# First stage of a three-block layer: modulation columns split between TensorE sums up front and VectorE sums beside the projections

## Chip, cores, metric

One core of one Trainium2 chip runs the whole program once. The metric is device microseconds of that execution (lower is better); the number compared is the median of several executions.

## What is computed

The reference is a long layer in float32 on 1024 tokens of width 1024. Only its beginning matters here: an adaptive norm whose shifts, scales and gates are columns of one product, the input projections, a gated linear attention, and later a second norm and a feed-forward part that use the remaining columns.

```python
def adaln(cond, w, b):
    return jax.nn.silu(cond) @ w + b          # w: 1024 x 6144, b: 6144
...
sh1, sc1, gt1, sh2, sc2, gt2 = jnp.split(adaln(c, w_ada, b_ada), 6, axis=-1)
csh1, csc1, ... = jnp.split(adaln(c_ctx, w_ada, b_ada), 6, axis=-1)   # only these two are used
hc = modulate(rmsnorm(ctx, g_pre_mix), csh1, csc1)      # h * (1 + scale) + shift; ctx: 256 tokens
hx = modulate(rmsnorm(x, g_pre_mix), sh1, sc1)
yx = token_mixers(hx @ w_in, ...)                       # projections, gates, linear attention
x = x + gt1 * rmsnorm(yx @ w_out, g_post_mix)
hx = modulate(rmsnorm(x, g_pre_ffn), sh2, sc2)
x = x + gt2 * rmsnorm(conv_ffn(hx, ...), g_post_ffn)
```

Two further blocks (windowed attention with a recurrent mixer, and a mixture of experts) follow and are not touched.

## The kernel before

The program is a row of stages. A stage gives each engine its instruction list; it ends when every engine has ended its list, and the next begins then. Within a stage the engines are ordered by semaphores that are waited for by hand-written counts. Each engine runs its list in order, and DMAs are issued from the lists of SyncE (SP) and ScalarE (ACT) in order too.

**`stage_modulation` (L228).** All 6144 columns of the product are made, spread over the 128 partitions, in `mod_rows`: eight rows of 1024, named `R_SH1, R_G1, R_GP1, R_SH2, R_G2, R_GP2, R_CSH, R_CG`. `w_ada` comes in 12 chunks of 512 columns (2 MB each, `ada_weights`, four buffers). Partition p holds eight of the 1024 input rows, `k` = 0 to 7. For each chunk VectorE forms a chain over `k` = 0 to 6 (L341 once, L345 six times), ScalarE scales the eighth part (L296), and TensorE sums over the partitions with an all-ones matrix and adds the bias (L373, L374, L375: three float32 matmuls with 512 moving columns, the last with one row). ScalarE copies the result from PSUM (L302). The first four chunks are done twice, for `c` and for `c_ctx` (L323). SP reloads a buffer when its `sum_mm` count is there. ScalarE's queue brings in the masks, the small parameters, `ctx`, `x` and four gain rows (L293). At the end TensorE turns the parameters (L398), VectorE copies them (L353) and multiplies the gains into five rows (L359, L362).

**`stage_norm_turn` "norm1" (L403)** normalises ten tiles of tokens and turns them with TensorE; it begins when the first stage has ended.

**`stage_project_mix` (L535).** First 40 steps `q` (five groups of eight): SP loads a 128 x 512 slice of `w_in` (`w_tm`, L594, two buffers; load `q` waits for `tm_low` of `q-2`), ScalarE and VectorE split it in a high and a low part (L208, L213), and TensorE does 12 matmuls with it (6 in the third group, which has two token tiles). In steps 9 to 12, 17 to 20 and 25 and 26, VectorE also copies a finished tile from PSUM (L684). Then 17 kinds `n` of 128 output columns each (`w_cm`, L601, one buffer), with 48 matmuls of 512 columns per kind for the later ones. PSUM banks 6 and 7 are unused by kinds 5 and later.

**`stage_gates` (L735), `stage_gla` (L857).** The second runs two context chunks and then eight chunks of `x` in a loop. Between them, VectorE updates the states (L950) and stages `q_chunk` and `k_chunk` (L966, L967), for which TensorE waits.

Of the kernel before, what the change touches and what calls it, by code (L numbers as in the profile page):

```python
# [17 lines left out]
ALU = mybir.AluOpType  # L18
ACT = mybir.ActivationFunctionType
AX = mybir.AxisListType.X  # L20
P = 128
# [3 lines left out]
D = 1024  # L25
# [202 lines left out]
def stage_modulation(core):  # L228

# [6 lines left out]
    csil = core.at("cond_silu", 108.25, [P, 2, KD])  # L238
    ones = core.at("ones", 109, [P, P])
    scaled = [core.at(f"scaled_rows{n}", kb, [P, 512]) for n, kb in enumerate((110, 202))]  # L240
    bias = core.at("ada_bias", 178, [1, 6 * D])
    SUMMED = KD - 1
    graw = core.at("gain_rows", 150, [P, 4, D])
# [3 lines left out]
    with Stage(core, "mod") as s:  # L247
        (masks_in, x_in, ctx_in, cond_in, param_in, bias_in, gain_in, silu_done, zeroed, params_turned,
         params_out, rows_done, ctx_rows_done, combined, order, sum_mm, ctx_sum, ctx_mm) = s.sems(
            "masks_in", "x_in", "ctx_in", "cond_in", "param_in", "bias_in", "gain_in", "silu_done",  # L250
            "zeroed", "params_turned", "params_out", "rows_done", "ctx_rows_done", "combined", "order",
            "sum_mm", "ctx_sum", "ctx_mm")
        scaled_done = s.sem("scaled_done")
        w_in = [s.sem(f"w_in{j}") for j in range(NW)]
        summed = [s.sem(f"summed{j}") for j in range(NW)]
        n_par = sum(len(t) for t in PARAM_ROWS)

        @s.b.gpsimd
        def _(pool):
            nc.gpsimd.memset(ones[:], 1.0).then_inc(zeroed, 1)  # L260

        @s.b.sync
        def _(sp):
            with nc.allow_non_contiguous_dma(reason="short vectors"):
                for v, name in enumerate(("c", "c_ctx")):
                    src = dram[name].rearrange("a d -> (a d)") if name == "c" else dram[name]
                    sp.dma_start(cvec[:, v, :], src.rearrange("(p k) -> p k", k=KD)).then_inc(cond_in, 16)
            sp.dma_start(bias[:], dram["b_ada"]).then_inc(bias_in, 16)

            def load(i, before):  # L270
                for j in range(NW):
                    if before is not None:

                        sp.wait_ge(sum_mm, before * NW + (j + 1))
                    sp.dma_start(ada_w[:, j], dram["w_ada"][0].rearrange("(p k) n -> p k n", k=KD)
                                 [:, :, bass.ds(i * (512 * NW) + 512 * j, 512)]).then_inc(w_in[j], 16)
            run_loop(sp, 3, load)

        @s.b.scalar
        def _(act):  # L280
            act.wait_ge(cond_in, 32)
            nc.scalar.activation(csil[:], cvec[:], ACT.Silu).then_inc(silu_done, 1)
            act.dma_start(core.masks.ap().rearrange("p a b -> p (a b)"), dram["masks"]).then_inc(masks_in, 16)
# [6 lines left out]
            act.dma_start(core.ctx[:], dram["ctx"][0].rearrange("(t p) d -> p t d", p=P)).then_inc(ctx_in, 16)  # L290
            act.dma_start(core.x0[:], dram["x"][0].rearrange("(t p) d -> p t d", p=P)).then_inc(x_in, 16)
            for g, name in enumerate(("g_pre_mix", "g_post_mix", "g_pre_ffn", "g_post_ffn")):
                act.dma_start(graw[:, g, :], dram[name].to_broadcast([P, D])).then_inc(gain_in, 16)  # L293

            def scale(j, v, n):
                nc.scalar.activation(scaled[n][:], ada_w[:, j, SUMMED], ACT.Copy,  # L296
                                     scale=csil[:, v, SUMMED:SUMMED + 1]).then_inc(scaled_done, 1)

            def take(i, j):

                act.wait_ge(sum_mm, i * NW + j)
                nc.scalar.activation(flat_rows[:, bass.ds(i * (512 * NW) + 512 * (j - 1), 512)],  # L302
                                     ps[:, (j - 1) % NW, :], ACT.Copy).then_inc(rows_done, 1)

            def evacuate(i, before):
                for j in range(NW):
                    act.wait_ge(w_in[j], i * 16 + 16)
                    if before is None:
                        if j == 0:
                            act.wait_ge(silu_done, 1)  # L310
                        else:

                            act.wait_ge(sum_mm, j)
                        scale(j, 1, 0)
                        scale(j, 0, 1)
                    else:
                        act.wait_ge(sum_mm, i * NW + (j - 1 if j else 0))
                        scale(j, 0, j % 2)
                    if before is not None or j:
                        take(i, j)  # L320
                    if before is None:
                        act.wait_ge(ctx_mm, j + 1)
                        nc.scalar.activation(flat_rows[:, 6 * D + 512 * j:6 * D + 512 * j + 512],  # L323
                                             ps[:, 4 + (j + 1) % 4, :], ACT.Copy).then_inc(ctx_rows_done, 1)
            run_loop(act, 3, evacuate)
            take(3, 0)

        @s.b.vector
        def _(dve):
            dve.wait_ge(silu_done, 1)  # L330

            def sums(i, before):
                for j in range(NW):
                    dve.wait_ge(w_in[j], i * 16 + 16)
                    chains = [(0, flat_rows[:, bass.ds(i * (512 * NW) + 512 * j, 512)], summed[j])]
                    if before is None:
                        chains.insert(0, (1, flat_rows[:, 6 * D + 512 * j:6 * D + 512 * j + 512], ctx_sum))
                    for n, (v, acc, done) in enumerate(chains):
                        m = SUMMED - 1
                        at = m * (2 * j + n) if before is None else i * (m * NW) + (m * NW + m * j)  # L340
                        nc.vector.tensor_scalar(acc, ada_w[:, j, 0], csil[:, v, 0:1], None, ALU.mult  # L341
                                                ).then_inc(order, 1)
                        for k in range(1, SUMMED):
                            dve.wait_ge(order, at + k)
                            nc.vector.scalar_tensor_tensor(out=acc, in0=ada_w[:, j, k], scalar=csil[:, v, k:k + 1],  # L345
                                                           in1=acc, op0=ALU.mult, op1=ALU.add
                                                           ).then_inc(order if k < SUMMED - 1 else done, 1)
            run_loop(dve, 3, sums)

            dve.wait_ge(params_turned, 1)  # L350
            for t, parts in enumerate(PARAM_ROWS):
                n = sum(x[2] for x in parts)
                nc.vector.tensor_copy(core.pcol[:, t * P:t * P + n], ps[:, 7, t * P:t * P + n]).then_inc(params_out, 1)  # L353
# [2691 lines left out]
```

## Time and profile before

| | |
|---|---|
| median of 3 runs | 3918.95 us (3918.48 to 3922.56) |
| profiled execution | 3924.63 us, its span 3922.8 us |
| TensorE busy / VectorE busy | 81% / 55% of the span |
| mean granted TensorE clock | 0.885 of 2.4 GHz |
| `stage_modulation` | 0 to 119.7 us |
| norm1 | 119.7 to 163.65 us |
| `stage_project_mix` | 163.65 to 476.2 us |
| gates, then `stage_gla` | 476.2 to 520.9, 520.9 to 604.2 us |

Times inside the trace count from the first instruction of the span. A float32 matmul stands in the trace as two records. A granted clock of 1.00 is 2.4 GHz and 0.50 is 1.2 GHz.

### The profile page before, as it was taken

Reading aid. Unit: us, or ns where it says so; the run is one execution under the profiler, and the core shown is the slowest. Engines: PE = TensorE matmul, PEld = TensorE weight load, DVE = VectorE, ACT = ScalarE, POOL = GpSimd, SP = SyncE. Lnnn points to the kernel's source line nnn. Section 1 sums busy time; section 2 is a strip of 40 time slices with the busy share of each in tenths; the row PEclk is TensorE's granted clock in tenths of the full one; section 3 lists DMA queues with packets and bytes.
Section 4 is the critical chain, followed back from the end, with each engine's and each line's share of the span. In section 5 each row is a group of like instructions: output and inputs, shape, how many; then the busy total and the mean of one; then the engine's idle time right before and its main releaser. Section 6 shows DMA issues by size and latency. Waiting matters only on the chain. (4 is left out here: it accounts for less than half of the span.)

```text
span 3922.8 us, 58296 instructions
## 1 busy us (share of the span) xinstructions
PE 3194.4 (81%) x24517; PEld 2476.0 (63%) x24517; DVE 2172.2 (55%) x2577; ACT 1343.7 (34%) x1777; POOL 423.9 (11%) x256
## 2 busy tenths in 40 slices
PE   6699957589999898777686876769699982999995
PEld 1478745478888676654382754638466671888884
DVE  7632254456666333363674747657311238888885
ACT  1321143312121222354242423324210121777774
POOL 0200011300000010211121202112000000121210
PEclk8699977789999999898797887879799985999997
DMA  8131103111111322102001010100311224999996
GB/s 330 47 92 46 30 1 113 59 54 49 48 49 36 140 85 98 43 17 77 1 4 61 3 63 1 46 18 4 114 33 37 108 108 151 359 399 398 396 396 214
DMA packets 219994, 424.20 MB, mean 108 GB/s; under 512 B 13120, under 2 KB 122642, under 8 KB 219538
## 3 DMA queue, kind: packets, MB, share of 16 engines
q1 hardware_dynamic: 212434, 394.75, 28.1%
q0 software_dynamic: 4608, 16.78, 1.7%
q10 hardware_dynamic: 2753, 9.66, 0.6%
q8 instruction: 168, 2.75, 0.3%
q14 instruction: 31, 0.25, 0.0%
HBM read 387.61 MB, written 33.55 MB: 107 GB/s over the span
## 5 line engine op out<-in xcount | busy, mean ns | idle before, releaser
L213 DVE TENSOR_TENSOR w_exp_low<-w_exp,w_exp_high 128x2048 fp32r<-128x2048 f32 x192 | 438.0, 2291 | 56.6 <-ACT w_exp_high L208 56.5
L208 ACT ACTIVATE w_exp_high<-w_exp 128x2048 fp32r<-128x2048 f32 x192 | 367.9, 1919 | 126.2 <-PE psum L221 126.2
L219 PE MATMUL psum<-ffn_high,w_high 128*128 128x512 f32 x704 | 274.7, 390 | 9.0 <-DVE w_low L213 9.0
L220 PE MATMUL psum<-ffn_low,w_high 128*128 128x512 f32 x704 | 274.6, 390 | 0.0
L221 PE MATMUL psum<-ffn_high,w_low 128*128 128x512 f32 x704 | 274.4, 390 | 0.0
L1375 DVE SCALAR_TENSOR_TENSOR ffn_hidden<-u_padded,param_columns,ffn_hidden 128x1024 f32 (+1 forms) x176 | 226.2, 1285 | 23.8 <-DVE ffn_hidden L1375 0.2
L219 PE MATMUL psum<-w_exp_high,x_turned_high 128*128 128x512 f32 x512 | 204.0, 398 | 7.0 <-DVE w_exp_low L213 7.0
L1853 PE MATMUL psum<-mixers_hT,w_rkv 128*128 128x512 f32 x384 | 176.6, 622 | 37.7 <-DMA w_rkv<-in_w_in 37.7
L221 PE MATMUL psum<-w_exp_high,x_turned_low 128*128 128x512 f32 x512 | 201.3, 393 | 0.0
L220 PE MATMUL psum<-w_exp_low,x_turned_high 128*128 128x512 f32 x512 | 200.9, 392 | 0.0
L2288 DVE COPY inverse<-psum 64x512 f32<-64x512 f32 x192 | 121.8, 637 | 74.3 <-PE psum L2123 48.9
L1853 PEld LDWEIGHTS psum<-mixers_hT,w_rkv 128*128 128x128 f32 x384 | 76.5, 201 | 135.4 <-issue 96.1
L219 PE MATMUL psum<-ffn_down_w_split,ffn_down_lhs_split 128*128 128x512 f32 x352 | 140.4, 399 | 22.8 <-DVE ffn_down_lhs_split L213 17.2
L219 PEld LDWEIGHTS psum<-ffn_high,w_high 128*128 128x128 f32 x704 | 132.6, 188 | 36.8 <-DVE w_low L213 9.4
L2222 ACT ACTIVATE inverse<-psum 64x512 f32<-64x512 f32 x192 | 106.9, 557 | 131.7 <-PE psum L2123 105.8
L221 PEld LDWEIGHTS psum<-ffn_high,w_low 128*128 128x128 f32 x704 | 132.6, 188 | 27.6
L220 PEld LDWEIGHTS psum<-ffn_low,w_high 128*128 128x128 f32 x704 | 132.6, 188 | 27.5
L2557 DVE TENSOR_TENSOR gates_sb<-gates_sb,psum 128x1024 f32<-128x1024 f32 x16 | 19.5, 1221 | 232.7 <-PE psum L2505 232.7
L513 PE MATMUL psum<-masks,norm_h 128*128 128x128 f32 x272 | 60.2, 397 | 102.3 <-POOL norm_h L502 63.9
L213 DVE TENSOR_TENSOR ffn_down_w_split<-ffn_down_ring,ffn_down_w_split 128x1024 fp32r<-128x1024 f32 x44 | 53.9, 1225 | 158.1 <-ACT ffn_down_lhs_split L208 158.1
L220 PE MATMUL psum<-ffn_down_w_split,ffn_down_lhs_split 128*128 128x512 f32 x352 | 139.5, 396 | 0.0
L221 PE MATMUL psum<-ffn_down_w_split,ffn_down_lhs_split 128*128 128x512 f32 x352 | 139.5, 396 | 0.0
(435 smaller groups left out, 7822.3 us busy)
## 6 DMA issues: line engine op xcount, KB each, us to landing
w_exp<-in_exp_w_gate SPq DMA_DIRECT2D x32, 2048.0 KB, 11.3
w_exp<-in_exp_w_up SPq DMA_DIRECT2D x32, 2048.0 KB, 11.1
w_exp<-in_exp_w_down SPq DMA_DIRECT2D x32, 2048.0 KB, 11.4
ada_weights<-in_w_ada SPq DMA_DIRECT2D x12, 2048.0 KB, 14.4
w_raw<-in_w_up SPq DMA_DIRECT2D x44, 512.0 KB, 3.7
ffn_down_ring<-in_w_down SPq DMA_DIRECT2D x44, 512.0 KB, 3.5
mix_out_ring<-in_w_out SPq DMA_DIRECT2D x32, 512.0 KB, 3.6
mixers_hT<-hidden SPq DMA_DIRECT2D x4, 4096.0 KB, 13.2
```

Source lines behind the costliest of these rows:

```text
L208: return nc.scalar.activation(out, src, ACT.Copy, scale=scale)
L213: return nc.vector.tensor_tensor(out, src, high.bitcast(F32), ALU.subtract)
L219: nc.tensor.matmul(out, left[0], right[0], start=start, stop=False)
L220: nc.tensor.matmul(out, left[0], right[1], start=False, stop=False)
L221: return nc.tensor.matmul(out, left[1], right[0], start=False, stop=stop)
L513: ins = nc.tensor.transpose(ps[:, 2 * (t % 4) + k // 4, (k % 4) * P:(k % 4 + 1) * P], hbuf[:, t % SLOTS, k * P:(k + 1) * P], core.mask(M_ID))
L1375: ins = nc.vector.scalar_tensor_tensor(out=out, in0=src, scalar=weight, in1=out, op0=ALU.mult, op1=ALU.add)
L1853: ins = nc.tensor.matmul(ps[:, 2 * m + h, :], w[n][:, kt], hT[:, kt, 512 * h:512 * h + 512], start=(kt == 0), stop=(kt == KD - 1))
L2222: nc.scalar.activation(place[rows[1], :], ps[rows[1], inverse_bank(n, 1), columns], ACT.Copy).then_inc(inv_lower[n % 2], 1)
L2288: nc.vector.tensor_copy(place[rows[0], :], ps[rows[0], inverse_bank(n, 0), columns]).then_inc(inv_upper[n % 2], 1)
L2557: nc.vector.tensor_tensor(sg[:, h], sg[:, h], ps[:, 4 * h + 2:4 * h + 4, :], ALU.mult).then_inc(parts, 1)
```

## The change

The first stage makes only the 2048 columns of the first norm (`R_SH1`, `R_G1`, `R_CSH`, `R_CG`). For each of four chunks TensorE does eight accumulating float32 matmuls whose stationary operand is two columns wide (`c` and `c_ctx`) and whose moving operand is a 128 x 512 slice of the weights; the result is two rows of 512. VectorE adds the bias, and two float32 matmuls with a two-row selection matrix (2 x 128, moving operand 2 x 512) spread the rows over the partitions; they come one chunk late in TensorE's queue, the last pair behind the transposes of the parameters. ScalarE copies the shift rows, VectorE takes the scale rows from PSUM with the gain in four `scalar_tensor_tensor` of 128 x 512 (`gains(2)`, `gains(3)`). `x` and `ctx` are loaded on SP behind the four chunks, three gain rows and the three products with them move to `stage_gla`, between the context chunks and the loop. The other 4096 columns are summed in `stage_project_mix`: 16 halves of 1 MB are loaded on SP between the `w_in` loads, VectorE adds 64 products of 128 x 512 into `mod_rows` (the schedule is `room`), and after kinds 5 to 12 TensorE sums each block over the partitions with one float32 matmul, which ScalarE copies. The bias now lies in row 0 of the accumulator, which POOL clears first. `room` puts no product in steps 0 to 4 and 16 to 25, one in 8 to 12 and 26 to 28, two in 5 to 7, 13 to 15 and 29 to 39, and four in each of kinds 0 to 4, two in kind 5.

```diff
 def stage_modulation(core):
+            for j in range(NW):
+                sp.dma_start(ada_w[:, j], dram["w_ada"][0].rearrange("(p k) n -> p k n", k=KD)
+                             [:, :, 512 * j:512 * j + 512]).then_inc(w_in[j], 16)
+            sp.dma_start(core.x0[:], dram["x"][0].rearrange("(t p) d -> p t d", p=P)).then_inc(x_in, 16)
+            sp.dma_start(core.ctx[:], dram["ctx"][0].rearrange("(t p) d -> p t d", p=P)).then_inc(ctx_in, 16)
...
+            dve.wait_ge(masks_in, 16)
+            for v in range(2):
+                nc.vector.tensor_copy(select[:, v, :], core.masks[0:2, M_ID, v:v + 1].to_broadcast([2, P])
+                                      ).then_inc(selects, 1)
...
+            for j in range(NW):
+                dve.wait_ge(pair_mm, j + 1)
+                nc.vector.tensor_tensor(pairs[:, j], ps[0:2, j, :], bias[:, 512 * j:512 * j + 512], ALU.add
+                                        ).then_inc(pair_done, 1)
+            dve.wait_ge(gain_in, 16)
+            gains(2)
+            gains(3)
...
+            for j in range(NW):
+                pe.wait_ge(w_in[j], 16)
+                for k in range(KD):
+                    ins = nc.tensor.matmul(ps[0:2, j, :], csil[:, k, :], ada_w[:, j, k], start=(k == 0),
+                                           stop=(k == KD - 1))
+                ins.then_inc(pair_mm, 1)
+                if j:
+                    spread_rows(j - 1)
...
+            spread_rows(NW - 1)
 def stage_project_mix(core):
+    room = [0] * 5 + [2] * 3 + [1] * 5 + [2] * 3 + [0] * (KD + 2) + [1] * 3 + [2] * (3 + KD) + [4] * (irregular + 1)
...
+            nc.gpsimd.memset(flat_rows[:, ADA:ADA + 4 * D], 0.0).then_inc(rows_zero, 1)
...
+            def load_ada(step):
+                for h in ada_loads.get(step, ()):
+                    if h >= 2:
+                        sp.wait_ge(ada_used, h - 1)
+                    first = ADA + 512 * (h // 2)
+                    sp.dma_start(ada_w[:, h % 2], dram["w_ada"][0].rearrange("(p k) n -> p k n", k=KD)
+                                 [:, 4 * (h % 2):4 * (h % 2) + 4, first:first + 512]).then_inc(ada_in[h % 2], 16)
...
+                if n in sums_at:
...
+                    pe.wait_ge(ada_used, 2 * m + 2)
+                    nc.tensor.matmul(ps[:, 6 + m % 2, :], core.ones[:], flat_rows[:, first:first + 512], start=True,
+                                     stop=True).then_inc(ada_sum, 1)
...
+            def modulate(step):
...
+                    ins = nc.vector.scalar_tensor_tensor(out=acc, in0=ada_w[:, h % 2, k], scalar=core.csil[:, n, 0:1],
+                                                         in1=acc, op0=ALU.mult, op1=ALU.add).then_inc(ada_order, 1)
 def stage_gla(core):
+            for g, name in enumerate(("g_post_mix", "g_pre_ffn", "g_post_ffn")):
+                sp.dma_start(graw[:, g, :], core.dram[name].to_broadcast([P, D])).then_inc(gain_in, 16)
...
+            dve.wait_ge(gain_in, 48)
+            nc.vector.tensor_tensor(rows[:, R_GP1], rows[:, R_GP1], graw[:, 0], ALU.mult)
+            nc.vector.scalar_tensor_tensor(out=rows[:, R_G2], in0=rows[:, R_G2], scalar=1.0, in1=graw[:, 1],
+                                           op0=ALU.add, op1=ALU.mult)
+            nc.vector.tensor_tensor(rows[:, R_GP2], rows[:, R_GP2], graw[:, 2], ALU.mult)
             run_loop(dve, TT // 2, step)
```

The loads of halves 0 and 1 come behind the `w_in` load of step 1, the others behind steps 9, 12, 16, 18, 31, 33, 35, 37, 39 and kinds 2, 4, 5, 6 and 7.

## Rows read from the trace of the kernel before

**Rows 1.** Windows by stage: engine busy us (instructions), granted clock, DMA share, GB/s.

```profile
0.00:119.70 119.70, 73.11 (x99) 22.39 (x99) 85.42 (x120) 21.02 (x35) 0.41 (x5) 0.78 0.77 283
119.70:163.65 43.95, 19.68 (x80) 15.68 (x80) 35.94 (x40) 23.40 (x41) 23.49 (x10) 0.50 0.00 0
163.65:476.16 312.51, 298.66 (x1320) 246.04 (x1320) 83.58 (x92) 52.11 (x70) 0.00 (x0) 0.97 0.23 63
```

**Rows 2.** Timeline of the end of the first stage: start, us, engine, line.

```profile
112.40 0.49 PE L398 MATMUL psum<-masks,param_rows 128*128 128x128 f32 x3
...
112.92 0.61 DVE L353 COPY param_columns<-psum 128x128 f32<-128x128 f32 x3 [3.81 <-PE psum L398]
113.44 3.48 DVE L359 SCALAR_TENSOR_TENSOR mod_rows<-mod_rows,gain_rows 128x1024 f32<-128x1024 f32 x3
116.85 2.35 DVE L362 TENSOR_TENSOR mod_rows<-mod_rows,gain_rows 128x1024 f32<-128x1024 f32 x2
119.70 1.28 ACT L431 ACT_TABLE_LOAD   x1 [6.59 <-PEq L185]
```

**Rows 3.** Groups of VectorE in the first stage.

```profile
L345 DVE SCALAR_TENSOR_TENSOR mod_rows<-ada_weights,cond_silu,mod_rows 128x512 f32<-128x512 f32 (+1 forms) x96 | 72.2, 752 | 3.4
```

**Rows 4.** DMA view, 0 to 60 us: GB/s in 40 slices, issues with KB, us to landing.

```profile
GB/s 0 22 108 358 369 404 381 385 371 385 406 404 399 407 399 397 397 410 407 399 397 396 407 399 408 396 406 404 378 388 390 385 384 392 385 382 390 390 240 188
```

**Rows 5.** Timeline: VectorE's first instruction on chunk 0.

```profile
15.97 0.49 DVE L341 TENSOR_SCALAR mod_rows<-ada_weights,cond_silu 128x512 f32<-128x512 f32 x1 [15.97 <-DMA ada_weights<-in_w_ada]
```

**Rows 6.** Timeline of TensorE: float32 matmuls in a chain, at either clock.

```profile
23.93 2.05 PE L373 MATMUL psum<-mod_rows,ones 128*128 128x512 f32 x2 [23.93 <-ACT scaled_rows L296]
...
31.49 1.79 PE L374 MATMUL psum<-scaled_rows,ones 128*128 128x512 f32 x2
33.21 1.12 PE L375 MATMUL psum<-ada_bias,ones 1*128 1x512 f32 x2
...
82.89 1.02 PE L374 MATMUL psum<-scaled_rows,ones 128*128 128x512 f32 x2
83.84 1.12 PE L375 MATMUL psum<-ada_bias,ones 1*128 x2
...
479.68 13.16 PE L780 MATMUL psum<-gate_low,w_gates 32*128 32x256 f32 x18 [5.12 <-DMA w_gates<-in_w_ab]
```

**Rows 7.** The same engine later: eight records, that is four float32 matmuls.

```profile
2809.92 3.59 PE L2505 MATMUL psum<-rwkv_out_cm,w_projections 128*128 128x512 f32 x8
2813.35 3.60 PE L2505 MATMUL psum<-att_out_cm,w_projections 128*128 128x512 f32 x8
```

**Rows 8.** Windows inside a stage, columns as in Rows 1: TensorE's clock.

```profile
60.64:80.88 20.24, 19.11 (x22) 5.36 (x20) 19.39 (x29) 3.62 (x6) 0.00 (x0) 0.50 0.61 215
80.88:89.00 8.12, 7.11 (x15) 2.23 (x14) 6.21 (x10) 2.33 (x4) 0.00 (x0) 1.00 1.00 344
479.70:492.80 13.10, 13.10 (x18) 5.80 (x18) 6.01 (x4) 7.84 (x7) 0.00 (x0) 0.50 0.00 0
```

**Rows 9.** Windows in the projections, columns as in Rows 1.

```profile
212.00:233.00 21.00, 18.36 (x75) 13.16 (x75) 9.93 (x15) 6.80 (x11) 0.00 (x0) 1.00 0.45 124
233.00:271.00 38.00, 38.00 (x169) 31.49 (x168) 10.29 (x15) 10.31 (x18) 0.00 (x0) 1.00 0.34 93
282.00:476.00 194.00, 191.15 (x864) 158.55 (x863) 47.51 (x40) 19.55 (x19) 0.00 (x0) 1.00 0.16 41
```

**Rows 10.** Timeline of ScalarE and VectorE in the projections' steps.

```profile
173.77 0.63 ACT L208 ACTIVATE w_tm_split<-w_tm 128x512 fp32r<-128x512 f32 x1 [5.27 <-PE psum L221]
...
193.49 0.69 DVE L213 TENSOR_TENSOR w_tm_split<-w_tm,w_tm_split 128x512 fp32r<-128x512 f32 x1 [2.03 <-ACT w_tm_split L208]
194.10 0.68 DVE L684 COPY v_tm<-psum 128x512 f32<-128x512 f32 x1
196.21 0.69 DVE L213 TENSOR_TENSOR w_tm_split<-w_tm,w_tm_split 128x512 fp32r<-128x512 f32 x1 [1.43 <-ACT w_tm_split L208]
```

**Rows 11.** DMA view, 163 to 470 us: loads, KB each, us to landing.

```profile
w_tm<-in_w_in SPq DMA_DIRECT2D x40, 256.0 KB, 2.6
w_cm<-in_w_in SPq DMA_DIRECT2D x17, 512.0 KB, 3.7
```

**Rows 12.** Timeline of the linear attention between context chunks and loop.

```profile
529.94 1.12 DVE L950 SCALAR_TENSOR_TENSOR state<-state,chunk_decay,psum 128x128 f32<-128x128 f32 x4 [2.50 <-PE psum L995]
...
530.98 0.30 DVE L966 COPY q_chunk<-q_decayed 128x256 f32<-128x256 f32 x1
...
531.94 2.08 PE L1018 MATMUL psum<-q_chunk,k_chunk 64*128 64x128 f32 x16 [2.04 <-DVE k_chunk L967]
```

More of the change, by code:

```diff
@@ L237, in stage_modulation @@
     cvec = core.at("cond_vectors", 108, [P, 2, KD])
[L238 to L243, printed above, removed]
+    csil = core.csil = core.at("cond_silu", 10, [P, KD, 2])
+    ones = core.ones = core.at("ones", 9, [P, P])
+    select = core.at("select_row", 109, [2, 2, P])
+    pairs = core.at("row_pairs", 178, [2, NW, 512])
+    bias = core.at("ada_bias", 186, [2, 2 * D])
+    graw = core.at("gain_rows", 150, [P, D])
     praw = core.at("param_rows", 166, [P, 3, P])
@@ L289, in _ @@
                     at += n
[L290 to L324, printed above, removed]
@@ L325, in _ @@
-            run_loop(act, 3, evacuate)
-            take(3, 0)
+            for j in range(2):
+                for v in range(2):
+                    act.wait_ge(spread, 2 * j + v + 1)
+                    nc.scalar.activation(place(j, v), ps[:, spread_bank(j, v), :], ACT.Copy).then_inc(shifts_done, 1)
         @s.b.vector
         def _(dve):
[L330 to L347, printed above, removed]
@@ L348, in _, with gains @@
-            run_loop(dve, 3, sums)
+            dve.wait_ge(masks_in, 16)
+            for v in range(2):
+                nc.vector.tensor_copy(select[:, v, :], core.masks[0:2, M_ID, v:v + 1].to_broadcast([2, P])
+                                      ).then_inc(selects, 1)
+            dve.wait_ge(bias_in, 16)
+            def gains(j):
+                for v in range(2):
+                    dve.wait_ge(spread, 2 * j + v + 1)
+                    first = 512 * (j - 2)
+                    nc.vector.scalar_tensor_tensor(out=place(j, v), in0=ps[:, spread_bank(j, v), :], scalar=1.0,
+                                                   in1=graw[:, first:first + 512], op0=ALU.add, op1=ALU.mult
+                                                   ).then_inc(gains_done, 1)
@@ L392, in _, with spread_rows @@
-            run_loop(pe, 3, products)
+            def spread_rows(j):
+                pe.wait_ge(pair_done, j + 1)
+                if j >= 2:
+                    pe.wait_ge(shifts_done, 2 * j - 2)
+                for v in range(2):
+                    nc.tensor.matmul(ps[:, spread_bank(j, v), :], select[:, v, :], pairs[:, j], start=True, stop=True
+                                     ).then_inc(spread, 1)
+            pe.wait_ge(silu_done, 1)
+            pe.wait_ge(selects, 2)
+            for j in range(NW):
[6 more added lines that the diff above has]
+                    spread_rows(j - 1)
@@ L575, in stage_project_mix @@
         tm_in = (tm_in0, tm_in1)
+        ada_in = [s.sem(f"ada_in{j}") for j in range(2)]
+        rows_zero, bias_in, ada_order, ada_used, ada_sum, ada_out = s.sems(
+            "rows_zero", "bias_in", "ada_order", "ada_used", "ada_sum", "ada_out")
+        sums_at = range(irregular, irregular + HALVES // 2)
         first_tile = [sum(len(g[1]) for g in groups[:n]) for n in range(len(groups) + 1)]
```

115 lines of the change are left out of this document (64 added, 51 removed).

## The prediction, made before the changed kernel was run

> **What bounds the kernel now.** I read the windows by stage first, then the timeline of the first stage and of the places that the change touches. The first stage takes 119.7 us, while TensorE is busy for 73 and VectorE for 85 of them [rows 1]. VectorE's share is almost all L345, 96 instructions of 752 ns [rows 3]. From 3.5 us on the DMA engines move some 390 GB/s [rows 4]; the 34 MB that the stage moves (119.7 us at 283 GB/s) would take 87 at that rate, so neither the engines nor the DMA fill the stage: load, chain, sum and evacuation of four buffers wait for each other. The last part is serial: transposes at 112.4, three copies, five products with gains, end at 119.2, next stage at 119.7 [rows 2]. Norm1 begins only then, so every microsecond off this stage is a microsecond off the run. The projections are different: from 282 to 476 us TensorE is busy for 191 of 194, and in 233 to 271 for all of 38 [rows 9]. Work added there is free on VectorE, ScalarE and the DMA while it stays in their gaps, and is paid in full on TensorE. In the linear attention TensorE waits 2.04 us for VectorE's staging between the context chunks and the loop [rows 12]: what is put ahead of that staging is paid in full too.
>
> **The first stage after the change.** When does chunk 0 land? Before, VectorE starts on it at 15.97 us [rows 5]. Summing the 1.5 us slices to there gives 4.6 MB [rows 4]; 2.1 MB are chunk 0, so 2.5 MB of ScalarE's inputs shared the engines with it. After the change ScalarE's queue holds about 1.8 MB (masks 1.1, one gain row 0.5, small ones 0.2), so 3.9 MB have to pass: 0.7 MB less at 0.39 MB/us, 14.2 us; if the small loads are issued too slowly to take their share, 13.3. I take 14.0. Later chunks follow every 5.4 us (2.1 MB), at 19.4, 24.8 and 30.2; `x` and `ctx`, 5.2 MB, land at 43.6. The masks, which VectorE needs for the selection, come ahead of chunk 0.
>
> From 14.0 us TensorE does 32 float32 matmuls of 512 columns for the pairs, 8 for the spreading, and 3 transposes. One costs 0.86 us at 2.4 GHz (four in 3.43 us, [rows 7]; 0.95 with changing 128-column weights, 82.89 to 83.84 in [rows 6]). At 1.2 GHz it is 1.75 us: L780 needs 13.16 us for what is 7.5 matmuls of 512 columns [rows 6]. The first chain is slower than the loads, so TensorE sets the end at either clock, and which clock it gets decides the size of the gain.
>
> What the rows show of that clock: TensorE was busy for 19.1 of 20.2 us from 60.6 on, with one matmul of three using a single row, and stayed at 1.2 GHz; with the same mixture it was back at 2.4 in the next window [rows 8]. In L780, 32 rows of the array, it was busy without a gap for 13.10 us and stayed at 1.2 GHz [rows 8]. Being busy is thus not enough here; matmuls that use a small part of the array did not bring the clock up. The new chain uses all 128 rows but two of 128 columns, and the spreading uses two rows. No row shows a chain of so few columns. I take the likeness to L780: 1.2 GHz through the stage. The other end is 2.4 GHz after a start at 1.2; a chain on the full array rose between 23.9 and 33.2 us, when a matmul fell from about 1.9 to 1.1 us [rows 6].
>
> Sum at 1.2 GHz: 14.0 + 32 x 1.75 = 56.0, + 8 x 1.8 = 14.4 for the spreads, + 0.9 for the transposes at half speed (0.49 at full [rows 2]) = 85.3. Behind the last spread come one gain instruction (0.8, as L345 in [rows 3]), three copies (0.6 [rows 2]) and semaphores (0.2): 86.9 against 119.2 before, **32.3 us saved**. The bias additions (2 x 512, at most 0.7 each as the PSUM copies in [rows 10]) lie under TensorE's next chunk, and `x` at 43.6 is covered; uncovered they would cost nothing until 87. Without the last two products and the first three the tail of 5.8 us is gone, which is in the sum.
>
> **The projections.** Eight float32 sums over the partitions go into TensorE's full queue. 8 x 0.95 = **7.6 us**, bounds 6.9 (0.86 each) and 8.5. The 64 products take VectorE 64 x 0.75 = 48 us. A step is 2.72 us (193.49 to 196.21 in [rows 10]); the split takes 0.69 and a copy 0.68. Two products more make 2.3 us, one and a copy 2.2, so each fits before the next split, which begins 2.03 us after the one before has ended. In the kinds four products are 3.2 us of at least 10.8 (48 matmuls at 0.225, 38 us for 169 in [rows 9]). What is queued behind them is the next split, for which TensorE has 1.3 us of reserve per step (split ready 1.4 us into a step of 2.72).
>
> The loads: a `w_tm` load lands after 2.6 us [rows 11] and is wanted 4.1 us after it can be issued (it is issued when the low part of two steps earlier has ended, and its own high part begins 1.35 us before two steps are over), so it has 1.5 us of reserve. A 1 MB half ahead of it takes the engines 2.7 us at 390 GB/s; the next `w_tm` is issued 2.7 us later and finds some 0.6 us left. That fits, except in the third group (212 to 233 us), where TensorE already idles 2.6 of 21 us [rows 9] behind loads: halves 4 and 5 go out there, about 0.8 us. In steps 31 to 39 a half, from 256 and 512 KB in 2.6 and 3.7 us [rows 11] worth 5 to 6 us, is wanted 5.4 us after its issue: VectorE may wait up to 1 us, five times, which uses up the reserve. At the start, two halves stand ahead of `w_tm` 2, 2.6 MB with the first slices; flowing from 165.7 at 390 GB/s they and `w_tm` 2 are through at 173.1, and its split is due at 173.77 [rows 10]. The clearing by POOL hides under the 5 us before that load is issued. For all of this **1.3 us**, bounds 0 and 5.
>
> **The linear attention.** Three products of 128 x 1024 at 1.15 us (3.48 us for three, [rows 2]) stand ahead of `q_chunk`: **3.5 us**. The gains' loads, 1.5 MB issued ten us before they are wanted (520.9 to 531.0), should be there; 3 us more if not.
>
> **Sum.** -32.3 + 7.6 + 1.3 + 3.5 = -19.9 us. From the profiled span, 3922.8, that is 3902.9; this execution took 3924.63, 5.7 above the median, so I take the difference over to the median: 3918.95 - 19.9 = **3899**. Its own range is 3893 to 3907 (chunk 0 0.7 earlier, matmuls of 1.71, sums of 0.86, no stalls at one end; 5 us of stalls and late gains at the other).
>
> **Rivals.** (1) *The clock rises in the first stage.* Five us at half speed cost 2.5; then 14.0 + 2.5 + 27.5 (32 x 0.86) + 7.6 + 0.5 + 1.6 = 53.7, a saving of 65.5 and, less 12.4, 53.1: 3866 (3858 to 3875). For it: all 128 rows stream without a pause from 14 us on, and full-array chains rose within ten. Against: L780 and 60.6 to 80.9 [rows 8]. The Trainium skill, "TensorE: Matmul & The Clock Gate", Part 1, says that throttling is the default and sustained activity releases it, going by how busy TensorE is; by that rule this would be the outcome, but the two stretches above do not agree with it when busy is all that counts. (2) *It ends slower: VectorE's products hold up the splits in the steps.* Place: steps 5 to 39, 42 products. If the schedule fitted nowhere and each were paid on TensorE's path, 42 x 0.75 = 31.5 us plus 42 short idles in which the clock falls, some 10 more, the run would be at 3899 + 41 = 3940. It turns slower once the projections lose more than 21 us, that is over half a microsecond in each step; the gaps of 2.03 us [rows 10] speak against it. (3) *The stage is still held by loads.* If `x` and `ctx` came behind everything at half the rate, 80 us, they would still be under TensorE's 85; so with the low clock the change of the load order is worth nothing by itself, and the time stays 3899. With the high clock it would cost the difference to 54, 26 us: 3892.
>
> **Chances.** Low clock as summed 0.62; clock up 0.28; loads or a partly raised clock in between (3875 to 3892) 0.05; stalls that eat the gain 0.05. The range must reach into the clock-up case: 3861 to 3907. What a measurement of this kernel can tell from no change is about 0.2%, 8 us. Faster than 3911: 0.93; within: 0.04; slower: 0.03.
>
> **What would show it.** Granted clock of 0.50 from 14 to 85 us and pair matmuls (two records) 1.7 us apart: right; 0.86 us apart: rival 1. End of the first stage, norm1's table load at 87.4 instead of 119.7. The projections 9 us longer than 312.5; waits of the splits for `ada_weights` or of ScalarE for `w_tm` longer than before mean rival 2. TensorE's 2.04 us wait in the attention grows to 5.5. The prediction is most likely wrong through the clock, next through the load order.

## The result, and the profile after

The changed kernel takes **3868.86 us** (median of 4 runs, 3867.81 to 3874.81) against 3920.76 for the kernel before on the same chip (3918.48 to 3924.49): a ratio of 0.987, 95% interval 0.9853 to 0.9887, or some 51 us less. The prediction was 3899, and its rival 1, with TensorE's clock up in the first stage, gave 3866. The profiled execution took 3874.81 us with a span of 3872.9, so the two profiled spans differ by 49.9. The variants below ran in three later groups, in which the kernel before took 3921.86, 3920.59 and 3923.89 us; every ratio is to the kernel before of its own group. Two executions, 4756.03 us of room15 and 10182.41 us of four_edits, are far above all others of the same kernel and are left out of the medians.

Windows by stage of the changed kernel: first stage, norm1, projections, gates, linear attention. The columns are those of [rows 1] (window, its length, busy us and instructions of PE, PEld, DVE, ACT and POOL, granted clock, DMA share, GB/s).

```profile
0.00:56.97 56.97, 38.15 (x83) 8.39 (x83) 6.34 (x13) 3.89 (x7) 0.41 (x5) 0.99 0.74 271
56.97:100.94 43.97, 19.69 (x80) 15.69 (x80) 35.96 (x40) 23.41 (x41) 23.51 (x10) 0.50 0.00 1
100.94:425.94 325.00, 307.34 (x1336) 249.58 (x1336) 128.74 (x156) 56.00 (x78) 3.51 (x1) 0.97 0.36 112
425.94:470.37 44.43, 17.79 (x24) 7.63 (x24) 33.57 (x24) 26.13 (x21) 1.76 (x4) 0.52 0.00 1
470.37:556.31 85.94, 61.33 (x584) 52.38 (x584) 33.07 (x108) 26.34 (x66) 11.61 (x20) 0.81 0.05 19
```

Against [rows 1] the first stage is 62.7 us shorter, norm1 the same, the projections 12.5 longer (325.00 against 312.51), the gates 0.5 shorter (44.91 before) and the attention 2.9 longer (83.11 before). That is 47.9 less. The later stages, which the change doesn't touch, differ by up to 3 us each in both directions and come to 2.0 less in this pair of profiles; the same scatter is in the profiles of every kernel below, so less than 2 to 3 us of a whole time can't be assigned to a cause. The projections scatter too. Six variants below leave their code as it is (x_on_act, rows32, rows64, rows96, rows32_x_on_act, products_in_loop), and their profiles have 324.45 to 328.55 us for the stage; the kernel before has 312.5 and, in the profile of before_bias128, 312.7. So the 12.5 us are one draw of 11.9 to 16.1. Finer than that only those differences can be read that come back at the same step in all seven profiles.

Timeline of the first stage: start, us, engine, line.

```profile
17.30 16.18 PE L338 MATMUL psum<-ada_weights,cond_silu 128*2 128x512 f32 x32 [17.30 <-DMA ada_weights<-in_w_ada]
33.40 1.98 PE L331 MATMUL psum<-row_pairs,select_row 2*128 2x512 f32 x4
35.31 7.03 PE L338 MATMUL psum<-ada_weights,cond_silu 128*2 128x512 f32 x16
42.27 1.98 PE L331 MATMUL psum<-row_pairs,select_row 2*128 2x512 f32 x4
44.18 7.03 PE L338 MATMUL psum<-ada_weights,cond_silu 128*2 128x512 f32 x16
...
53.47 1.98 PE L331 MATMUL psum<-row_pairs,select_row 2*128 2x512 f32 x4
...
56.97 1.28 ACT L381 ACT_TABLE_LOAD   x1 [12.08 <-PEq L185]
```

Sixteen records are the eight float32 matmuls of a chunk. Chunks 2 and 3 take 6.9 us each, 0.86 a matmul, which is 2.4 GHz; chunks 0 and 1 take 16.1 together, 2.3 more, because the first 4.6 us ran at half that. From 17.30 us TensorE never waits for a load again: the stage is its chain, started by the landing of chunk 0. The column of the granted clock has to be read with care here. It shows 1.00 until the first change that the trace records, even where the matmuls are 0.85 us a record apart instead of 0.43; in the first stage I therefore go by the length of the groups.

The waits in the projections: us in all, times and longest; the last line is the kernel before, for comparison with the first:

```profile
ACT w_tm_split L208 <- DMA w_tm<-in_w_in: 28.8, 12, 7.6
DVE mod_rows L690 <- DMA ada_weights_late<-in_w_ada: 29.0, 10, 6.6
PE psum L219 <- DVE qT L721: 2.6, 1, 2.6
...
ACT w_tm_split L208 <- DMA w_tm<-in_w_in: 17.6, 11, 2.3
```

Timeline in the projections' steps 15 and 16, then at the first sum over the partitions, and between the attention's context chunks and its loop:

```profile
152.68 0.75 DVE L690 SCALAR_TENSOR_TENSOR mod_rows<-ada_weights_late,cond_silu,mod_rows 128x512 f32<-128x512 f32 x1 [3.62 <-DMA ada_weights_late<-in_w_ada]
153.35 1.32 DVE L213 TENSOR_TENSOR w_tm_split<-w_tm,w_tm_split 128x512 fp32r<-128x512 f32 x2
...
297.23 1.02 PE L628 MATMUL psum<-mod_rows,ones 128*128 128x512 f32 x2
...
480.27 1.23 DVE L1006 TENSOR_TENSOR mod_rows<-mod_rows,gain_rows_late 128x1024 f32<-128x1024 f32 x1
481.43 1.21 DVE L1007 SCALAR_TENSOR_TENSOR mod_rows<-mod_rows,gain_rows_late 128x1024 f32<-128x1024 f32 x1
482.56 1.21 DVE L1009 TENSOR_TENSOR mod_rows<-mod_rows,gain_rows_late 128x1024 f32<-128x1024 f32 x1
483.69 0.28 DVE L989 COPY q_chunk<-q_decayed 128x256 f32<-128x256 f32 x1
...
484.63 2.08 PE L1046 MATMUL psum<-q_chunk,k_chunk 64*128 64x128 f32 x16 [5.45 <-DVE k_chunk L990]
```

In step 15 VectorE stands 3.62 us at a product whose half has not landed, and the low parts of two splits go out behind it one after the other: TensorE's operands are late for it. In the attention three products stand ahead of `q_chunk`, and TensorE's wait is 5.45 us where it was 2.04 [rows 12].

### The profile page after: what moved, and what is told of

Its sections match the earlier page's. It is cut to its first block and busy times, and to the rows that moved or that the text cites. A ratio compares the mean times of both kernels' runs of the same rounds, so it can differ in the third digit from the quotient of the medians.

```text
span 3872.9 us, 58111 instructions
## 1 busy us (share of the span) xinstructions
PE 3165.9 (82%) x24517; PEld 2461.5 (64%) x24517; DVE 2139.4 (55%) x2537; ACT 1330.9 (34%) x1757; POOL 432.3 (11%) x257
## 6 DMA issues: line engine op xcount, KB each, us to landing
w_exp<-in_exp_w_gate SPq DMA_DIRECT2D x32, 2048.0 KB, 11.9
w_exp<-in_exp_w_down SPq DMA_DIRECT2D x32, 2048.0 KB, 12.5
```

## Theories

The part of the gain that was not predicted is the clock. **Theory R**: what keeps TensorE at 1.2 GHz while it is busy is that matmuls use few rows of the array; two columns are enough to bring it up. **Its rival B**: being busy brings it up, whatever part of the array is used, and the stretches of [rows 8] stayed low for another reason. For the 12.5 us of the projections the theory has three parts: each sum over the partitions costs its 0.9 us (7.2 in all), a product that waits for its half stands ahead of the splits (theory V in the expectations below), and the first two halves delay `w_tm` 2. The rival (theory D) is that the DMA engines are simply full.

## Experiments

**32 and 64 rows in the pairs** (labels rows32, rows64: the products of 96 or 64 partitions are left out)

```diff
-... matmul(ps[0:2, j, :], csil[:, k, :], ada_w[:, j, k], ...
+... matmul(ps[0:2, j, :], csil[0:32, k, :], ada_w[0:32, j, k], ...
```

> The changed kernel, with each of the 32 pair matmuls over the first 32 rows of the array only (the products of the other 96 partitions are left out of the first norm's columns). Number of matmuls, columns, loads and waits are as before. Theory R (rows): TensorE's clock stays at 1.2 GHz under a chain that uses few rows, whatever its columns; then the granted clock is 0.50 from 17 us to the end of the stage, pair matmuls are 1.7 us apart, the first stage ends at 88 to 90 us instead of 57.0, and the run takes 3899 to 3903 us. Theory B (busy): any chain without pauses raises the clock, and what held it down in L780 and from 60.6 to 80.8 us of the kernel before was something else; then the stage ends at 57 and the run takes 3869 us.

> The same with 64 rows (the products of the other 64 partitions are left out). Theory R does not say on which side 64 rows fall: the stage ends at 57 or at 88 us, and shows it. Theory B: 57 us, 3869 us in all.

With 32 rows 3906.16 us (ratio 0.9966, 0.9954 to 0.9979), with 64 one run of 3906.16. Timeline of TensorE with 32 rows:

```profile
15.68 27.46 PE L338 MATMUL psum<-ada_weights,cond_silu 32*2 32x512 f32 x32 [15.68 <-DMA ada_weights<-in_w_ada]
43.07 3.78 PE L331 MATMUL psum<-row_pairs,select_row 2*128 2x512 f32 x4
46.77 13.81 PE L338 MATMUL psum<-ada_weights,cond_silu 32*2 32x512 f32 x16
```

The same instructions, just as busy, take 13.81 us a chunk instead of 7.03, to the end of the stage, which is 86.92 us long (86.38 with 64 rows). The first rise of the clock that the trace records is in the projections, at 140.09 us. B falls, R stands, though the time is 3 us above the 3899 to 3903 that the expectation gave for R. The area of the array in use does not explain it either: L780, with 32 rows by 128 columns, stayed low [rows 8], and 128 rows by 2 columns, a smaller area, came up. This is also the mechanism of the forecast made real: it forecast a stage end 32.3 us earlier and the table load at 87.4; here they are 32.0 us and 87.67. That they agree so closely is partly luck: chunk 0 starts TensorE at 15.68 us and not at 14.0, and the chain from there to the table load is 71.99 us where the forecast's terms make 73.4 (a pair matmul costs 1.71 us and not 1.75).

**96 rows** (label rows96: the products of 32 partitions are left out; the same edit with 96)

> Pair matmuls on 96 of the 128 rows (the products of 32 partitions are left out). 32 and 64 rows left TensorE at 1.2 GHz for the whole stage, 128 let it rise within 5 us. If the rows count in proportion, 96 rises too but later, with a stage between 56 and 87 us; if only a full array counts, the stage is 86.9 us as with 32.

One run, 3877.92 us, stage 60.09. The clock rises 5.7 us after the first matmul, and falls for 3.4 us 0.4 to 0.8 us behind each of the first two spreads of two-row matmuls. Windows of that kernel, columns as before:

```profile
21.00:34.66 13.66, 13.66 (x32) 2.88 (x31) 1.36 (x2) 1.19 (x2) 0.00 (x0) 1.00 1.05 395
34.66:38.07 3.41, 3.41 (x5) 0.52 (x4) 0.00 (x0) 0.00 (x0) 0.00 (x0) 0.50 1.02 408
38.07:44.90 6.83, 6.83 (x17) 1.59 (x16) 0.68 (x1) 0.99 (x2) 0.00 (x0) 1.00 0.71 284
44.90:48.31 3.41, 3.41 (x6) 0.53 (x5) 0.00 (x0) 0.20 (x1) 0.00 (x0) 0.50 0.00 0
```

TensorE is busy in every microsecond of these, with five or six records in 3.41 us at the low clock and seventeen in 6.83 us at the high one. In the changed kernel, with 128 rows, the same spreads cost no fall. So neither of the two expectations held as written: 96 rows are between, and what the rows are mixed with counts.

**128 rows for the bias in the kernel before** (label before_bias128). The bias lies in row 0 of a cleared 128-row tile, so that the third matmul of each chain, one of a single row before, uses the array's full height.

```diff
-bias = core.at("ada_bias", 178, [1, 6 * D])
+bias = core.at("ada_bias", 178, [P, 6 * D])
+            nc.gpsimd.memset(bias[:], 0.0).then_inc(zeroed, 1)
...
-            sp.dma_start(bias[:], dram["b_ada"]).then_inc(bias_in, 16)
...
+            act.dma_start(bias[0:1, :], dram["b_ada"]).then_inc(bias_in, 16)
...
-nc.tensor.matmul(ps[:, bank, :], ones[0:1, :], bias_row,
+nc.tensor.matmul(ps[:, bank, :], ones[:], bias_row,
```

> The kernel before the change, with the bias in row 0 of a cleared 128-row tile, so that its 16 bias matmuls of the first stage use 128 rows instead of one; number and order of matmuls are the same. Theory R: the clock stays up once it has risen, through 60 to 81 us too, the first stage becomes 5 to 12 us shorter (VectorE's chains then set it), 3907 to 3914 us in all. Theory B: the clock falls and rises as before, 3919 us within 2.

3914.83 us, just over the 3907 to 3914 of R's expectation, ratio 0.998 (0.997 to 0.9989); the first stage is 111.44 us against 118.95, counted from its first instruction. The clock still falls, but mostly for 3.4 us at a time instead of the 20.24 in [rows 8]:

```profile
44.61:48.02 3.41, 3.41 (x5) 1.01 (x3) 3.27 (x5) 0.00 (x0) 0.00 (x0) 0.50 1.03 384
48.02:54.85 6.83, 3.96 (x9) 1.54 (x9) 6.54 (x11) 2.41 (x4) 0.00 (x0) 1.00 1.05 387
54.85:58.26 3.41, 3.41 (x5) 1.00 (x3) 3.27 (x5) 0.00 (x0) 0.00 (x0) 0.50 1.05 386
```

With 128 rows in each matmul the clock first rises 4.4 us after the first one (26.51 to 30.95 us), where it took 9.1 before (23.93 to 33.02), and the low stretches shrink, which only R expects. R's expectation that the clock stays up once risen was wrong. What the trace shows beside each of the six falls is a wait of TensorE of 2.3 to 3.1 us, in which the fall comes or within 0.8 us behind it; waits of 1.6 us and less have none. In the kernel before the falls come with waits too: the long stretch of [rows 8] begins at 60.33 us, 0.8 us behind a wait of 2.09. So the waits start a fall in both kernels, and what the rows change is how long the clock then stays down: 20.5 us with a single row in every third matmul, though TensorE was busy for 19.1 of 20.2 us, and 3.4 us in five of the six falls with 128 rows in all. Part of the 7.5 us can also be that the bias load moved to another queue; this run doesn't part the two.

**`x` and `ctx` on ScalarE's queue** (label x_on_act): only the load order is undone.

```diff
-            sp.dma_start(core.x0[:], ...)
-            sp.dma_start(core.ctx[:], ...)
+            act.dma_start(core.ctx[:], ...)
+            act.dma_start(core.x0[:], ...)
```

> The changed kernel with x and ctx loaded from ScalarE's queue behind the parameters, as in the kernel before, so that they share the DMA engines with chunks 1 to 3 instead of following them. If the order of the loads is part of the gain, chunks 2 and 3 land after TensorE wants them (35.3 and 44.2 us) and the stage ends up to 10 us later, 3879. If TensorE's chain alone sets the stage, the chunks are still in time or late by 1 to 2 us: 3869 to 3871.

3881.38 us (ratio 0.9902, 0.9886 to 0.9919), 12.5 above the changed kernel by the medians and 2 over the expectation's worst case. Timeline:

```profile
31.84 1.98 PE L331 MATMUL psum<-row_pairs,select_row 2*128 2x512 f32 x4
38.62 9.83 PE L338 MATMUL psum<-ada_weights,cond_silu 128*2 128x512 f32 x16 [4.80 <-DMA ada_weights<-in_w_ada]
```

Chunk 2 shares the engines with 5 MB and holds TensorE for 4.80 us. The granted clock is at half from 34.05 us, 0.2 us into that wait and right behind the spread, to 44.29, and the chunk takes 9.83 us instead of 7.03; which of the two, the wait or the two-row matmuls, brings the clock down isn't parted here. From the first pair matmul to norm1's table load it is 47.4 us (15.71 to 63.15) against 39.7 (17.30 to 56.97): 7.8 us in the stage. The other 4.7 us of the 12.5 are not seen in this pair of profiles (their projections are 324.45 and 325.00 us).

**The same at the low clock** (label rows32_x_on_act: products of 96 partitions left out)

> 32 rows for the pair matmuls (the products of 96 partitions are left out) and x and ctx on ScalarE's queue beside the chunks, as before the change. It tests what the prediction said of the load order: at 1.2 GHz, where a chunk's chain takes longer than its load, the order should be worth nothing, so the stage stays at 86.9 us; with 2.4 GHz the same move cost 6 to 9 us. If the loads hold the stage at the low clock too, chunk 2 at 38.6 us is late and the stage is longer by some microseconds.

One run, 3901.91 us. From the first pair matmul to the end it is 71.99 us (14.22 to 86.21) and with the loads in order also 71.99 (15.68 to 87.67). At 1.2 GHz the load order is worth nothing, as the prediction said; at 2.4 it is worth 8 us. The load order thus pays only with the higher clock.

**Room in step 15** (label room15). Half 4's first product, which stood in step 15, 3 us behind the issue of its load, moves to step 26 (`room` is the number of products in each step).

```diff
-... [1] * 5 + [2] * 3 + [0] * (KD + 2) + [1] * 3 + ...
+... [1] * 5 + [2, 2, 1] + [0] * (KD + 2) + [2, 1, 1] + ...
```

> The changed kernel with one product moved from step 15 to step 26 of the projections, so that VectorE asks for half 4 only there and not in step 15, where its load has just been issued; the loads are where they were. Of the 12.5 us that the projections got longer, 4.6 arise in steps 16 to 20. Theory V (VectorE stands 3.6 us in the wait for half 4, and the split of step 16 and the load of step 18 stand behind it): 3 to 4.5 us are gone, 3865 us. Theory D (the 1 MB halves 4 and 5 push back the small loads on the DMA engines): little changes, 3868 to 3869.

3872.77 us, ratio 0.9875 (0.9855 to 0.9895): in the time no gain, and the 3865 of theory V was missed. In the stage there is one. Measured at the first parts of the splits, the changed kernel loses 4.5 us against the kernel before between steps 15 and 24 (0.6 late at step 15, 5.1 at step 24), and this one 1.2 (0.3 and 1.5). The other profiles with the product in step 15 lose 3.9 to 4.7 us there, and three_edits and four_edits, where it has moved too, 1.5 and 1.1: theory V holds for this place, and the later places hide it in the time. At kind 5, where TensorE waits for the copy of `qT`, it loses 2.6 where the changed kernel loses 1.2. The projections take 322.72 us.

Kind 5 can be read closely. TensorE waits 1.4 us there in the kernel before, 2.57 in the changed kernel and 2.34 here. Behind the wait the granted clock stays up in the changed kernel; here it falls 1.2 us behind it. First the changed kernel from the end of its wait, then the fall here (columns as before):

```profile
286.26:289.67 3.41, 3.40 (x15) 2.86 (x16) 2.41 (x3) 0.00 (x0) 0.00 (x0) 1.00 0.37 78
...
281.12:284.53 3.41, 3.41 (x10) 2.67 (x9) 1.17 (x2) 0.00 (x0) 0.00 (x0) 0.50 0.73 210
```

The twelve profiles of the changed kernel and its variants fall into two sets by this. Six have no fall and lose 0.5 to 1.2 us at kind 5, which is the longer wait alone; six have one fall of 3.4 us and lose 2.3 to 3.2, which is the longer wait and 1.6 us more. At the first kinds the same thing works the other way: in or behind a wait of 3.2 us that every profile has, the clock is down for 6.8 us in the kernel before, and the variants gain nothing on it where it is as long, 1.1 us where it is 3.4 us (as in the changed kernel), and 2.6 where it does not fall.

**Halves 4 and 5 loaded in steps 24 and 26 as well** (label halves_late)

```diff
+    ada_loads = {{16: 24, 18: 26}.get(step, step): hs for step, hs in ada_loads.items()}
```

> The same, and halves 4 and 5 are loaded at steps 24 and 26 instead of 16 and 18, outside the third group where TensorE already waits for loads. Theory V: as room15, 3865. Theory D: only this one brings the 4.6 us back, 3864 to 3865, and is 3 to 4 us under room15.

3869.96 us (0.987, 0.9853 to 0.9886). Steps 16 to 24 are clean (from 1.2 us late to 1.4), and steps 25 to 29 lose 2.0: the loss has moved with the loads, and since the first product that wants half 4 now follows its load closely again, this does not part V from D. 324.33 us for the stage: nothing won.

**The eight sums behind the gates' projections** (label sums_in_gates). L628 and its copy leave the projections; in the gates TensorE is idle while VectorE and ScalarE work.

```diff
 def stage_gates(core):
+            for m in range(8):
+                if m >= 2:
+                    pe.wait_ge(ada_out, m - 1)
+                bank, row = ada_block(m)
+                nc.tensor.matmul(bank, core.ones[:], row, start=True, stop=True).then_inc(ada_sum, 1)
```

> The changed kernel with its eight late float32 sums over the partitions moved from kinds 5 to 12 of the projections to the end of TensorE's queue in the next stage (gates), in PSUM banks 3 and 7, and their copies into ScalarE's waits there. If a sum costs the projections 0.9 us because TensorE has no gap there, and the gates stage has 27 us of idle TensorE, the time falls by 6 to 7.3 us: 3862. If the copies delay VectorE's scans in the gates stage, that gives back up to 4.7 us (8 copies of 0.59): 3866.

3866.67 us (0.9864, 0.9844 to 0.9883), where 3862 was expected. Projections 317.12 us, 7.9 less; gates 44.82, 0.4 more. The 7.9 are not a clean price: the splits show where they come from. In the changed kernel the splits fall behind those of the kernel before by 0.9 us more with each of the kinds 5 to 12, 7.25 in all; here they stay 4.6 us behind (one 4.9). That is the price of the sums; the rest is mostly the first kinds (1.5 us gained) and kind 5 (1.2 lost), where the clock falls or does not.

**The gain products inside the attention's loop** (label products_in_loop): the four lines move from ahead of `run_loop` to behind the scores of its first chunk.

> The changed kernel with the three products with gain rows in the linear attention moved behind the first chunk's masked scores in VectorE's list, where VectorE waits 5 us for TensorE. If they cost 3.4 us because TensorE waits for the staging behind them, the time falls by 3 to 3.4 us: 3866. If TensorE's clock in the chunks that follow hangs on how long that pause is, the difference is smaller by what the clock gives back.

3868.36 us (0.9862, 0.9845 to 0.9878). TensorE's wait is back at its old length, and the attention at 82.45 us, 3.5 less:

```profile
482.50 2.08 PE L1047 MATMUL psum<-q_chunk,k_chunk 64*128 64x128 f32 x16 [2.04 <-DVE k_chunk L990]
```

The projections of this profile are 327.50 us, 2.5 more than in the other one, though nothing in them was changed: 1.2 more at the start (`w_tm` 2) and 1.5 more at kind 5, the same places where the other variants scatter. In the time no gain can be told.

**Three edits together, and a fourth** (labels three_edits, four_edits): room in step 15, sums in the gates, products in the loop; then also the first two halves loaded behind steps 2 and 3.

```diff
-    ada_loads = {0: [0, 1]}
+    ada_loads = {2: [0], 3: [1]}
...
-                    load_ada(0)
```

> Three of the edits above together: room for products in step 15, the eight sums moved behind the gates' projections, the three gain products inside the attention's loop. If their effects are independent, the stages should show what each showed alone: projections near 314 us (325.0 less 7.9 for the sums, less 3.4 for steps 16 to 20), gates 44.9, attention 82.5; together about 14 us less than the changed kernel, near 3855. If the later stages or the clock take part of it back, the stages show the 14 us and the time shows less.

> The same three edits, and the first two 1 MB halves issued behind w_tm 2 and 3 instead of ahead of w_tm 2. The third split then should not wait 7.6 us for w_tm 2: about 1 us less than three_edits in the projections if that wait is the cause (the third split came 1.5 to 2.7 us late in the variants so far), nothing if the halves only delay w_tm 4 and 5 instead.

Three: 3861.83 us (ratio 0.9837, 0.9824 to 0.985); four: 3858.11 (0.9838, 0.9824 to 0.9851). Windows of three_edits, projections to attention:

```profile
98.33:414.99 316.66, 299.51 (x1320) 246.48 (x1320) 128.74 (x156) 52.11 (x71) 3.51 (x1) 0.97 0.37 115
414.99:460.34 45.35, 28.99 (x40) 11.39 (x40) 33.58 (x24) 30.35 (x29) 1.76 (x4) 0.65 0.00 1
460.34:542.90 82.56, 61.30 (x584) 52.35 (x584) 33.10 (x108) 26.33 (x66) 11.60 (x20) 0.82 0.06 20
```

The stages give back 8.3 us in the projections and 3.4 in the attention and take 0.9 in the gates: 10.8 of the expected 14. Most of the rest is kind 5 again: this kernel loses 3.2 us there, with a fall of the clock, and arrives at it with 0.9. The fourth edit takes the wait for `w_tm` 2 away. ScalarE's third split, first without, then with it:

```profile
109.75 0.63 ACT L208 ACTIVATE w_tm_split<-w_tm 128x512 fp32r<-128x512 f32 x1 [7.35 <-DMA w_tm<-in_w_in]
```

```profile
108.19 0.63 ACT L208 ACTIVATE w_tm_split<-w_tm 128x512 fp32r<-128x512 f32 x1 [5.74 <-PE psum L221]
```

The projections are then 313.11 us, 0.6 from those of the kernel before, with the 16 halves and 64 products still beside them (the sums are in the gates), so full DMA engines were not what cost the changed kernel its 12.5 us. Of the 3.5 us that this profile is shorter than that of three_edits, 0.8 arise at the start, where the fourth edit acts (about 1 was expected), and 0.4 in steps 16 to 24; 2.3 come from the first kinds and kind 5, where nothing was changed. In the whole time they can't be told from the scatter (the two intervals are nearly the same). Both versions' intervals of ratios lie below the changed kernel's (0.9853 to 0.9887), by little, so they are taken as faster than it. By how much is less sure: three_edits by 7.0 us if the medians are compared, by 13 if the ratios 0.9837 and 0.987 are, and 10.8 us is what the stages show.

## Why the prediction was wrong, and where it was right

**The step that failed is "I take the likeness to L780: 1.2 GHz through the stage".** L780 and the new chain are alike in that each uses a small part of the array, but in different directions: 32 of 128 rows there, 2 of 128 columns here. The runs show that the rows decide. With 128 rows and 2 columns the clock rose 4.6 us after the first matmul; with 32 and 64 rows and the same 2 columns it stayed low for 70 us. The prediction had the right variable in hand (a single row in one matmul of three, [rows 8]) and wrote "a small part of the array" over it. It also took a chain of the first stage for one on the full array when it looked for the other end: its third matmul, L375, has a single row [rows 6]. The price of the step: 32 matmuls and 8 spreads at 0.86 and 0.95 instead of 1.75 and 1.8. From the first pair matmul to the table load it is 39.67 us in the changed kernel and 71.99 in rows32, 32.3 us; the ends of the stages differ by 30.7, since chunk 0 was later in the changed kernel, and the medians by 37.

By the busy-ness rule of the Trainium skill, "TensorE: Matmul & The Clock Gate", Part 1, the clock should rise in any sustained chain. It gives the right outcome for this change, and the wrong one for the 32- and 64-row variants, which were as busy: the measurement decides, and here the rule has to be read with the rows that a matmul uses.

**Rival 1's sum** put the end of the stage at 53.7 us; the table load came at 56.97. Chunk 0 was the difference: 17.3 us instead of 14.0. In six more profiles with the same first stage the table load comes between 53.75 and 56.60 us. Slow start 2.3 (forecast 2.5), matmuls at 0.86, spreads at 0.95 and the tail of 1.5 (1.6) were right. Over the ten profiles with the same loads in the same order chunk 0 started TensorE between 14.6 and 17.3 us, so this term moves by 2.7 us by itself and was later than forecast in all of them; in the changed kernel's profile it was at its late end. That the time came within 3 us of rival 1's 3866 is partly luck: the stage was 3.3 us longer than this sum and the projections 3.6 longer than theirs, and the scatter of the later stages, the gates and the attention took 3.1 back.

**The projections** lost 12.5 us where the sum had 8.9. The eight sums were right: the splits of the kinds come 0.905 us later each, 7.2 us for eight (forecast 7.6), and moved away they are gone. The stalls were mis-sized: 1.3 taken, 5.3 measured, just over the bound of 5. They are 0.6 at the start, which the prediction had found to fit by 0.7 us, 4.6 in steps 16 to 26, and 1.2 at kind 5, less 1.1 at the first kinds, where the clock came up sooner. (The start is read with care: the kernel before is itself 1.0 us later there in the profile of before_bias128, which has no halves.) The place of the 4.6 is the third group that it named, with the price of 0.8 us for the DMA alone. What it missed is the order on VectorE: half 4's first product stands in step 15, and its load is issued behind `w_tm` 16, at 146.08 us, only 3.0 us before VectorE gets to that product. A median half takes 6.2 us to land, so the product waits 3.62 us, and the splits of the next steps are queued behind it. For kind 5 the sum had no term: TensorE's wait for the copy of `qT` grew from 1.4 to 2.6 us.

**The attention** lost 2.9 (forecast 3.5): the three products were 3.5 us, as the wait's growth of 3.4 shows. The kernel before has 83.1 and 82.2 us for the stage in two profiles, so the 0.6 between the two figures is within its scatter.

**Rival 2** was right in kind and not in size: 4.6 us in some ten steps, not 31.5 in forty. **Rival 3**: the order is worth nothing at the low clock, as said (71.99 us both ways). At the high clock undoing it cost 8 us, not 26: `x` and `ctx` on the other queue share the engines with the chunks, they don't go ahead of all of them.

**Open** is what decides whether the clock falls behind a wait: at kind 5 it fell behind waits of 2.1 to 3.0 us in six profiles and stayed up behind 1.9 to 2.6 us in six others. Open are also the bias load's share in before_bias128, and the scatter of the later stages.

## What to carry to other kernels

Before forecasting TensorE's clock for a chain, sort the stretches of the trace by how many rows of the array their matmuls use, and not only by how busy they are. Here narrow outputs were harmless and short contractions were not, and a bias or broadcast matmul of one or two rows seems able to hold the matmuls around it down. When such a clock decides a stage, price each other part of the change at both clocks: the load order was worth nothing at one and 8 us at the other. When work is put ahead of an engine's urgent work, check for each piece that its data has been issued long enough before it, in the queue's own order, since one early instruction costs what is left of the landing, with all that is queued behind it. And before a stage's growth is put down to a change, compare several profiles in which that stage's code is the same, step by step: here it scattered by 4 us, mostly at its start and at two places where the clock may fall.

## What the runs showed of the hardware

- 128 rows by 2 columns, busy without a gap: up to 2.4 GHz after 4.6 us. 96 rows: up after 5.7, down for 3.4 us behind two groups of four two-row records. 64 and 32 rows: 1.2 GHz for 70 us and more.
- With all matmuls on 128 rows the clock also fell or in waits of TensorE of 2.1 to 3.2 us, not every time, and mostly for 3.4 us; at kind 5 such a fall cost 1.6 us.
- A one-row matmul made into one of 128 rows, with the rest of its rows zero, shortened the kernel before by 0.2% (its first stage by 7.5 us), though that matmul then covers 128 times the rows. A bias load that moved to another queue may have a part in it.
- The first chunk of 2 MB, with the same loads issued ahead of it, was there between 14.6 and 17.3 us in ten profiles.
